# Another order of the last sums with one tile's rows added on TensorE, and third buffers for a part of the fourth expert tile's weights

## What is computed

```python
def hier_moe(h, w_rg, b_rg, w_re, b_re, w1, w3, w2):
    ...                      # top-1 of 4 groups, then top-2 of its 4 experts: comb is 0 but for 2 experts
    for g in range(N_EXPERT_GROUPS):
        a = jnp.einsum('btd,edf->btef', h, w1[g])
        b = jnp.einsum('btd,edf->btef', h, w3[g])
        hid = jax.nn.silu(a) * b * comb[:, :, g, :, None]
        out = out + jnp.einsum('btef,efd->btd', hid, w2[g])
    return out

def decoder_layer(...):
    ...
    x = x + gt2 * hier_moe(h2, w_rg, b_rg, w_re, b_re, w1, w3, w2)

def rmsnorm(x, g):           # of the result, with normf_g: y_prompt and y_sample
    y = xf * lax.rsqrt(jnp.mean(xf * xf, axis=-1, keepdims=True) + RMS_EPS)
    return (y * g.astype(jnp.float32)).astype(x.dtype)
```

## Time and profile before

| | us |
|---|---|
| median of 3 runs | 1161.38 |
| lowest and highest | 1160.89, 1161.99 |
| the profiled execution | 1160.31 |
| its span (first to last instruction) | 1158.5 |
| PE, DVE, ACT, POOL busy in the span | 1107.6, 552.5, 361.5, 181.7 |

### The profile page before, as it was taken

One profiled execution on the slowest core, in us unless ns is written; L12 is line 12 of the kernel. 1 busy time (PEld: TensorE's weight loads), 2 busy tenths in 40 slices (PEclk: granted clock), 3 DMA queues, 4 the chain that ended last, 5 costly groups with the idle time before them and its releaser, 6 DMA issues.

```text
span 1158.5 us, 28784 instructions
## 1 busy us (share of the span) xinstructions
PE 1107.6 (96%) x12087; PEld 963.0 (83%) x12087; DVE 552.5 (48%) x1218; ACT 361.5 (31%) x658; POOL 181.7 (16%) x245
## 2 busy tenths in 40 slices
PE   4999999999999999999999999999999999999985
PEld 3899999999999998887789999999667768677741
DVE  1745565755556644553364434345763233223317
ACT  5623333433333323222244444423412111101112
POOL 1334243333330200000000000000020110111122
PEclk9999999999999999999999999999999999999988
DMA  9989989989968466556989778388769999999852
GB/s 353 344 273 347 336 317 385 346 320 334 356 249 292 132 227 232 212 206 250 380 323 335 281 268 304 91 252 336 296 247 358 422 419 410 418 404 420 351 186 78
DMA packets 164622, 350.19 MB, mean 302 GB/s; under 512 B 11595, under 2 KB 116219, under 8 KB 149998
## 3 DMA queue, kind: packets, MB, share of 16 engines
q1 hardware_dynamic: 151902, 325.06, 76.2%
q0 software_dynamic: 5808, 16.05, 3.9%
q10 hardware_dynamic: 6832, 7.93, 2.0%
HBM read 321.95 MB, written 115.14 MB: 377 GB/s over the span
## 4 chain that ended last, share of the span: by engine, by line
PE 89%; DVE 4%; issue 3%; SPq 2%; DMA 2%; ACT 1%; DVEq 0%; ACTq 0%
PE psum L983 48%; PE psum L1335 16%; PE psum L1347 7%; PE psum L1058 3%; PE psum L1044 2%; PE psum L1033 2%; PE psum L1024 2%; SPq L718 2%; PE psum L1080 2%; PE psum L906 1%; PE psum L1107 1%; DMA wraw<-in_w_in_dram 1%; PE psum L1004 1%; DMA adarB<-in_w_ada_dram 1%; PE psum L1422 1%
## 5 line engine op out<-in xcount | busy, mean ns | idle before, releaser
L983 PE MATMUL psum<-hHi,whi 128*128 128x272 f32 x1200 | 353.7, 295 | 0.3 <-ACT rb L1585 0.3
L983 PE MATMUL psum<-hLo,whi 128*128 128x272 f32 x1200 | 346.7, 289 | 0.0
L983 PE MATMUL psum<-hHi,wlo 128*128 128x272 f32 x1200 | 345.2, 288 | 0.0
L983 PEld LDWEIGHTS psum<-hHi,whi 128*128 128x128 f32 x1200 | 226.1, 188 | 12.0 <-issue 9.9
L983 PEld LDWEIGHTS psum<-hHi,wlo 128*128 128x128 f32 x1200 | 226.3, 189 | 0.0
L983 PEld LDWEIGHTS psum<-hLo,whi 128*128 128x128 f32 x1200 | 225.6, 188 | 0.0
L1335 PE MATMUL psum<-e,xs 128*32 128x256 f32 x3072 | 191.4, 382 | 14.7 <-issue 12.8
L1335 PEld LDWEIGHTS psum<-e,xs 128*32 128x32 f32 x3072 | 134.9, 110 | 65.4 <-issue 35.6
L1750 DVE TENSOR_TENSOR wlo<-wraw,whi 128x1024 fp32r<-128x1024 f32 x100 | 133.4, 1334 | 74.0 <-ACT whi L1487 73.3
L1487 ACT ACTIVATE whi<-wraw 128x1024 fp32r<-128x1024 f32 x100 | 105.0, 1052 | 34.6 <-PE psum L983 31.2
L2562 POOL DMA_INDIRECT xg<-x_tok,piece x45 | 42.8, 951 | 453.3 <-DVE piece L2269 248.0
(11 more groups left out here) (378 smaller groups left out, 1572.4 us busy)
## 6 DMA issues: line engine op xcount, KB each, us to landing
e<-in_w_dram SPq DMA_DIRECT2D x96, 1024.0 KB, 7.7
wraw<-in_w_in_dram SPq DMA_DIRECT2D x76, 512.0 KB, 6.6
out_dram<-in_cache_k_dram SPq DMA_DIRECT2D x32, 1022.0 KB, 9.6
out_dram<-in_cache_v_dram SPq DMA_DIRECT2D x32, 1022.0 KB, 8.0
adar<-in_w_ada_dram SPq DMA_DIRECT2D x36, 512.0 KB, 7.5
kvr<-in_cache_k_dram SPq DMA_DIRECT2D x8, 2048.0 KB, 7.8
kvr<-in_cache_v_dram SPq DMA_DIRECT2D x8, 2048.0 KB, 9.7
out_dram<-in_cache_k_dram SPq DMA_DIRECT2D x8, 1016.0 KB, 9.1
```

The source lines that it names most:

```text
L983: mm = pe.matmul(psum[:, t, 0:HALF], w[:, slot, k, :], x[:, k, cols], start=(k == 0 and n == 0), stop=(k == k_n - 1 and n == 2))
```

## The change

In the expert phase:
- There is a third buffer for W2 (`e2_2`) and one for the first half of W1 and W3 (`e13_2`), both for tile 3 alone. SP starts the load of `e2_2` right after W2 of tile 2, and that of `e13_2` when the slot table (`table_pe`) and the gather tables (`tab_done` 3) are made. Tile 3's second half of W1 and W3 is loaded as before.
- On PE, tiles 1 to 3 and the stages between are written out, and the loop begins at jp = 2. The stages come in the same order.
- SP's loop is turned: W2 of an odd tile stands at the head of the next pass. For tile 15 this load comes behind the loop, and there behind the stores of tile 14's rows, with the load of `place` behind it.
- DVE makes `gate_s`, `x2_s` and `fold4` (9 copies) between tile 0 and tile 1, ahead of the gather tables. They hold the sample tokens' gate and x2 in four blocks of 32 partitions by 256 columns, and a matrix that adds over the four blocks.
- Some small tables lie elsewhere in the memory.

In the tail:
- PE adds x2 to sum 4 (`residual(4)`) ahead of tile 15's outers and not at the end.
- Sum 3 gets its two gathered rows by PE (4 products with the identity) instead of DVE (`chosen_sum(0)` and `mixed(3)` are gone); its norm reads PSUM.
- The sample tokens' sum (sum 0) is made last but one and on 128 partitions x 256 columns. Its gate, sum and norm are on DVE and its squares are added over the blocks by PE (`fold4`); POOL has nothing left to do there.
- `NORM_ORDER` is sums 1, 2, 4, 0, 3. One of DVE's additions of `ya` moves behind the first `mixed`.

```diff
-NORM_ORDER = (1, 2, 0, 3, 4)
-PLACE_BANK = (0, 2, 6, 4, 0)
+NORM_ORDER = (1, 2, 4, 0, 3)
+PLACE_BANK = (2, 2, 6, 4, 0)
+MIXED = (1, 2, 4)
+SUMMED = {1: 1, 2: 2, 4: 3, 0: 4, 3: 5}
+FOLDED = 6
...
-            next_expert(1, 0, 2)
-            next_expert(1, 1, 3)
+            next_w13(1, 0, 2)
+            next_w2(1, 0, 2)
+            sp.wait_ge(xz_out, ZEROED + 16 * (TILES + 1))
+            for half in range(2):
+                sp.dma_start(half_lines(e2_2, half), half_source(w2_v, 3, half)).then_inc(e2_in[1], 16)
+            sp.wait_ge(table_pe, 1)
+            sp.wait_ge(tab_done, 3)
+            for n, w_v in enumerate((w1_v, w3_v)):
+                sp.dma_start(e13_2[:, n], half_source(w_v, 3, 0)).then_inc(e13a_in[1], 16)
+            sp.wait_ge(a_pe, 8 + 4)
+            load_e13(1, 3, 1)
...
-            with sp.Fori(2, pairs) as jp:
-                for q in range(2):
-                    next_expert(jp, q, sp.value_load(...))
-            sp.dma_start(place[:, :], k_small[0:TS, 96 + TS:96 + TS + NT]).then_inc(late_in, 16)
+            next_pair(2)
+            with sp.Fori(3, pairs) as jp:
+                next_w2(jp - 1, 1, expert(2 * jp - 1))
+                next_pair(jp)
             sp.wait_ge(ye_ev, 6 * before_last + 6)
...
+            next_w2(before_last, 1, expert(2 * before_last + 1))
+            sp.dma_start(place[:, :], k_small[0:TS, 96 + TS:96 + TS + NT]).then_inc(late_in, 16)
...
-            with pe.Fori(0, before_last) as jp:
+            outers(0, 1)
+            inners(0, 2)
+            outers(0, 2)
+            inners(0, 3, e13_2)
+            outers(1, 1, e2_2)
+            inners(1, 2)
+            outers(1, 2)
+            inners(1, 3)
+            with pe.Fori(2, before_last) as jp:
                 for u in (1, 2):
...
-            mixed(3, x2[:, 2, :], yc[:, 0, 0])
             chosen_sum(1)
-            normed(1)
-            root(0).then_inc(f_gate, 1)
             mixed(4, x2[:, 3, :], yc[:, 1, 0])
+            dve.wait_ge(y_pe, SUMMED[0])
+            own(dve.tensor_tensor(y_s[:, :], psum[:, PLACE_BANK[0], 0:DQ], gate_s[:, :], ALU.mult))
+            dve.tensor_tensor(y_s[:, :], y_s[:, :], x2_s[:, :], ALU.add).then_inc(f_gate, 1)
             normed(2)
+            normed(4)
+            root(0)
...
+            dve.scalar_tensor_tensor(y_s[:, :], y_s[:, :], rstd[:, TILES:TILES + 1], normf_s[:, :], ALU.mult, ALU.mult)\
+               .then_inc(f_y, 1)
             normed(3)
-            normed(4)
```

More of the change, by code:

```diff
@@ L1328, in _, with inner @@
             pe.sem_inc(ye_pe, 3)
-            def inner(q, g, half):
+            def inner(q, g, half, w13=None):
                 n_t = XT // 2
@@ L1417, in _ @@
                 residual(3, c, True)
+            pe.wait_ge(hT_done, 6 * before_last + 6)
+            for c in range(2):
+                residual(4, c, True)
             pe.wait_ge(e2_in[1], 32 * before_last + 32)
-            pe.wait_ge(hT_done, 6 * before_last + 6)
             for n in range(2):
@@ L2392, in tile, with evicted @@
                     placed()
-                    dve.wait_ge(g_done, 6 * jp + (3 * q + 1))
-                    for n in range(2):
+                    def evicted(n):
                         cols = slice(512 * n, 512 * n + 512)
@@ L2422, in _ @@
                 own(dve.tensor_copy(gate4[part, :], tokt[part, 2, DQ * n:DQ * n + DQ]))
+            for n in range(4):
+                part, cols = slice(32 * n, 32 * n + 32), slice(DQ * n, DQ * n + DQ)
+                own(dve.tensor_copy(gate_s[part, :], toks[:, 2, cols]))
+                own(dve.tensor_copy(x2_s[part, :], x2[0:NS, TILES, cols]))
+            own(dve.tensor_copy(fold4[:, :, :], fold[:, :].unsqueeze(1).to_broadcast([P, 4, 32])))
             own(dve.tensor_scalar(ntile[:, 6:7], ntile[:, 7:8], 2.0 * TS, -1.0 * TS, ALU.mult, ALU.add))
```

163 lines of the change are left out of this document (104 added, 59 removed).

## The result

The changed kernel takes **1153.71 us** in the median of 4 runs (1153.24 to 1155.36), against 1161.49 of the kernel before (4 runs, 1160.89 to 1161.99). The ratio is 0.9944, its 95% interval 0.9931 to 0.9957: faster by 0.43 to 0.69%, that is 5.0 to 8.0 us. Forecast were 3.9 us.

A forecast was written before the change was run, and what follows sets the result against it. PE, not the loads, was taken to pace the expert phase, and a chain of single steps the tail. Terms 0 + 0 + 0 - 3.9 us took the profiled 1160.31 to 1156.4, plus 1.07 to the median: 1157.5 us, range 1152.5 to 1162.5.

The forecast's parts named there:

- Third buffers, 0 us: Expert phase: loading 4 MB earlier gains nothing, as PE waits for no weights; at most 10.2 us if loads bound.
- slack of 15 us: Expert phase, tile 4: weights were taken to lie ready over 15 us before PE uses them, hiding the third buffers.
- Rival B: Expert phase: loads bound it after all, so the change gains 10.2 us more, 1147.3 us; chance 0.07.
- Written-out stages and turned loop, 0 us: Expert phase to tile 15: same products and order; W2 behind the stores still lands before the outers; no cost.
- Nine copies on DVE, 0 us: Ahead of the gather tables: some 2.8 us of copies delay tile 2's rows by 1.5 to 2.8 us, covered by 13.
- `residual(4)`, +1.7 us: Ahead of tile 15's outers: four new PE records come on top and start all of the tail 1.7 us later.
- D: Tile 15's inners: W2 slows the gathers, PE's standstill grows and its clock stays low longer, 1162 to 1166 us; chance 0.10.
- The tail behind the outers, -5.6 us: Second `yev` to last norm, reordered: with the +1.7 us of `residual(4)` included, the tail gains 3.9 us.
- rival E: Tail: the last norm hangs on ACT's and PE's chain, swallowing half the gain at 2 us more, 1159.2 to 1162; chance 0.15.
- The last store: End of the span: fewer stores ahead in its queue, at best 0.3 us gained; none counted.
- The bridge from the profiled execution to the median: Final sum: the median was put 1.07 us above the profiled execution, turning 1156.4 into 1157.5 us.
- Rival C: Tile 15's inners: gathers start later against PE, so more records run before the standstill, 1150 to 1155 us; chance 0.08.

The follow-up runs named there:

- w2_third: The changed kernel without the third buffer for W1 and W3, on a chip with 17.1 us tiles: 1154.56 us, ratio 0.9946 to the kernel before.
- again: The changed kernel once more, unaltered, on a chip with 15.54 us tiles: 1122.39 us, ratio 0.9931 to the kernel before.
- res_late: The changed kernel with PE's x2 products for sum 4 back at the end, not ahead of tile 15's outers: 1122.24 us, ratio 0.9931.
- before_w2_late: The kernel before with only tile 15's W2 and `place` moved behind the stores of tile 14's rows: 1160.17 us, ratio 1.0000.

## Why the prediction was right where it was, and where not

The direction and the cause, the new tail, were right, and the size was too small: 3.9 us forecast, 4.9 in the profiled pair, 5.0 to 8.0 in the runs.

**Third buffers, 0 us: right on such a chip.** Tiles stayed at 17 us at a DMA share of 1.02, and `w2_third` lost nothing. (My slack of 15 us was that of the first halves; the second halves of W1 and W3 started at 892.53, were there by 903.3 at the latest and had 11.) Rival B is out there: the share was full and the loads didn't bind. The Trainium skill's rule under "Perfetto Trace Analysis", section "Roofline", some 435 GB/s for the 16 engines of a core, fails to tell the two kinds of chip apart: the window shows 419 GB/s on one and 422 on the other, at the same share, and PE took 48.03 of 50 us in the one and all 50 in the other, with 10% more records (935 against 846).

**Written-out stages and turned loop, 0 us: right there, but not as a rule.** W2 behind the stores landed in time and made nothing longer. What I left out is the other side of this edit: W2 *ahead* of the stores holds them up. In the earlier trace rows the gathers started at +5.5, since W2 had been started by 1086.4 and with 10.3 us at most for a landing was there 7 us before the stores: nothing stood ahead of them. Where tiles take 15.54 us it's 6.4 us of delay, 2.2 us at the end of the tail and 0.15 to 0.3% of the time.

**Nine copies on DVE, 0 us: right.** Tile 2's rows were asked for at 866.27 instead of 863.41, 2.9 us later, within the 13 us of cover.

**`residual(4)`, +1.7 us: right where nothing disturbs it, not in the single trace.** It was +2.45 in one pair, +1.10 in the other and +1.74 where no standstill disturbs it (`again` +14.04, `res_late` +12.30). The extra comes from the first records after the standstill. In after the granted clock is 0.50 from 1120 to 1125, that is 1.2 GHz, and 1.00 from 1126 on; in before it is 1.00 from 1124 on. So in after the first two records of the residuals stand 1.02 and 0.68 us from the next, and in before 0.54 and 0.43, as on the chips without a standstill. That was D's warning, in small; its standstill didn't grow. D's premise was right, W2 and the gathers do slow each other (10.7 us to landing for 5.8), but its step from there was not: the standstill follows the issuing. And the term is no net price: `res_late` pays it at the end of the tail instead, with the same last norm.

**The tail behind the outers, -5.6 us (3.9 and 1.7): -6.7 measured.** This is the term that was mis-sized. Of the 1.1 us, half is on DVE: I added the lengths of rows, 1.22 for an addition and 1.28 for a norm, but the next row starts before the last one's end. In after's rows a norm's pitch is 1.21 (1146.60 to the reciprocal at 1147.81) and an addition from PSUM 1.14 (1143.09 to 1144.23). At the end of the sample tokens' norm DVE stands 0.6 us ahead of my plan. The other half is ACT's chain, 1.1 us ahead of it in the end: squares of `y_s` in 0.40 and not 0.53, the block sum's root at 1146.87, squares from PSUM in 1.01. So rival E, a late ACT chain, was wrong in sign; the last root was ready as DVE came to it.

**The last store, "at best 0.3, I count none": -0.73**, and the same on both kinds of chip (3.54 to 3.67 us are left behind the last norm in the kernels with the new tail, 3.02 in `res_late`, and 4.27 to 4.29 with the old one). A term whose best case I had named was more than twice as large, and most of it is another thing than I had named. Fewer transfers ahead give 0.38 (issue to landing 3.06 us before, 2.68 after). SP takes back 0.45: it starts the last store 0.48 us behind the last norm's end, when it has issued the four small ones, and before it was 0.03. The rest, 0.80, is POOL. Behind its last operation each engine has a row DRAIN, and the span's last rows come right behind the later of SP's and POOL's. POOL's, before and then after (shortest, median and longest in ns, first and last start in us), is

```profile
L536 POOLq DRAIN  x1: 9307/9307/9307, 1148.9 to 1148.9; - x1
```

```profile
L551 POOLq DRAIN  x1: 20299/20299/20299, 1110.7 to 1110.7; - x1
```

So in before it ends at 1158.25, 6.4 us behind the end of POOL's last operation (1151.86) and 1.0 us behind the last landing (1157.28), and the span ends 0.2 us later. In after POOL has no work in the tail, its DRAIN is over at 1131.0, and the span ends 0.4 us behind the last landing. My plan had counted what POOL's part cost DVE, and not this.

**The bridge from the profiled execution to the median** failed. The sum gives 4.9 by the terms that the traces measure, the medians 7.8. I had only the offset of before's trace to its median, 1.1 us, and took it for both kernels; after's lay 1.65 on the other side. That is 2.7 us. In the other pair of such traces `w2_third`'s profiled execution is its median, `before_w2_late`'s lies 1.2 below its own, and the medians differ by 5.6. With the rows that repeat (-6.72, -0.73) and the undisturbed +1.74 the sum is -5.7, within the result's interval of 5.0 to 8.0 and near the 5.6 of that pair. Whether more lies behind the 7.8 of the medians than four runs' scatter stays open.

**Rival C** didn't happen: the first gather came 0.8 us earlier and 142 instead of 152 records ran ahead of the standstill, but the residuals started where they had.

## What to carry to other kernels

A small store that others wait for belongs ahead of a bulk load in program order, even where the load's buffer is free earlier: 2 MB still under way ahead of it cost 6 us of landing. Whether that shows depends on how far the loads lag (on the chips with 17.1 us tiles W2 had landed, and the order was worth nothing) and on holes further on; a tail that has just been packed tightly loses the cover that the old one had, so look again at every arrival that the old hole hid. An engine that is off the chain can still end the span: look at when its last row ends. And a sum over one engine's rows should use the distance from start to start, while a forecast of a median needs the spread between executions, not the one that was profiled.

## What the chips showed that I had not expected

**The same kernel, 1161 or 1129 us.** On the chip of the result and on that of `w2_third` (it may be the same one) PE stops while indirect DMAs are under way, on three others it doesn't. In after, POOL issues nine gathers 1.25 us apart from 1107.16 on; PE's records come in groups of about four, 1.4 us apart, from 1111 to 1120. In the four traces with a standstill it begins 3.4 to 4.0 us after the issue of the first gather and ends 2.9 to 3.0 us after that of the last, whether that gather lands after 5.8 us or after 10.7. So its length goes with the issuing and not with the landing of the data; what PE stops on is not shown. Each tile's three gathers cost 1.5 us in the same way (17.1 against 15.54): in after three are issued from 1001.48 to 1003.98, and PE's records, else under 0.2 us apart, have gaps of 0.4 and 1.2 us at 1003.9 and 1004.6. The profile names nothing that PE waits for ("issue"). POOL's own rows are the same on both kinds, 0.94 us nearly all. What differs between the chips, none of the runs says; nor whether gathers started later would move the standstill to a cheaper place, which was not run on such a chip.

**A gain made of different parts.** With the standstill the tail is all of it by elimination (0.9944, with the moved W2 at 1.0000). Without it the tail alone gives 0.9974, and the moved W2 as much again. Both come to 0.993 to 0.9945, and a single ratio would have hidden that.
